# Sums of weight blocks made by accumulating transfers on GpSimd's queue instead of by VectorE

## The chip, the cores and the metric

One NeuronCore of a Trainium2 chip runs the whole program. The metric is the device time of one execution in microseconds (us), the median of three runs. Beside it stands one profiled execution with a time of its own. All data are float32. The core has TensorE (PE) for matrix products, VectorE (DVE), ScalarE (ACT) and GpSimd (POOL) for elementwise work, SyncE (SP) that issues most transfers, and 16 DMA engines that all queues of transfers share.

## What is computed

One decoder layer for 512 tokens of width 1024: half a SwiGLU, a mixer of gated linear attention and dilated attention, half a SwiGLU, and a last norm. The change touches the first two products of each SwiGLU only.

```python
def swiglu(x, w1, w3, w2):
    return (jax.nn.silu(x @ w1) * (x @ w3)) @ w2
x = x + 0.5 * swiglu(rms_norm(x, ffn1_norm[l]), ffn1_w1[l], ffn1_w3[l], ffn1_w2[l])
# ... mixer ...
x = x + 0.5 * swiglu(rms_norm(x, ffn2_norm[l]), ffn2_w1[l], ffn2_w3[l], ffn2_w2[l])
```

The hidden width is 2816, that is 22 tiles of 128 columns for `w1` and 22 for `w3`.

## The kernel before

**Units.** Weights come in units of [128 x 2048] float32, 1 MB each, into two buffers `raw0` and `raw1` that units use in turn. An "up" unit holds one 128-column tile of `w1` and one of `w3` for all 1024 inputs. Each float32 operand is split in a rounded part and the rest (`w_hi` by ACT, `w_lo` = raw - `w_hi` by DVE), and each product is three matmuls. A feed-forward layer runs in two parts of 12 and 10 up units, each followed by 8 "down" units.

**Seven-product units.** 35 of the 44 up units (the table `SEVEN`) are computed by a scheme of seven block products in place of eight. It needs sums of the token blocks, made once per layer (`tok_sums`), and for every such unit four sums of weight blocks. The unit's 2048 columns lie in `raw` as the blocks B22, B21, B11, B12, of 512 columns each. The sums are B22+B21, then that plus B11 (the near pair, for the unit's first side), and B11+B21, and the three-block sum plus B12 (the far pair, for its second side). In before, `add_blocks` makes all four on DVE from `raw`, into the spare columns of the tile `x`, one buffer for all units.

**Order around it.** A seven-product unit has two sides (halves), and `w_hi`, `w_lo` are double-buffered by side. PE works through seven terms of 12 matmuls; term 0 reads raw blocks of side 0 (`w_part`), term 1 is the first that reads sums (`w_split` of side 0), term 4 the first of side 1. While PE works on a unit, ACT and DVE prepare its side 1 and then side 0 of the next unit. For side 0 ACT rounds B11 and B12 (`round_raw`, L592) and the near sums (`round_sums`, L602); for side 1 it rounds B22 (L595) and the far sums (L602). DVE takes the differences (L1059, L1064, L1067), and each L1067 raises `w_split`. Between these, in fixed order on the same queues, ACT copies finished terms out of PSUM (`snap`, L704), and DVE forms gate and product (L1168 to L1187).

**Loads.** SP loads unit u when `w_split` says that unit u-2 is split on both sides, since it used the same `raw` buffer (L488). GpSimd has no transfers; it makes the rotary tables (L555 to L570, after the first 12 up units) and eight products in the mixer (L577).

## Time and profile before

| | us |
|---|---|
| median of 3 runs | 927.59 |
| lowest, highest | 927.41, 927.83 |
| profiled execution, first to last instruction (span) | 925.8 |
| PE busy | 917.7 |
| DVE busy | 676.5 |
| ACT busy | 463.9 |
| GpSimd busy | 49.2 |
| mean DMA rate | 103 GB/s |

Busy time of an engine tells how much it did, not whether anybody waited for it; matmul records overlap, since matmuls are pipelined. So the views that matter are who waited for whom, the rows in order of time inside a unit, and for transfers the time from issue to landing and the share of the 16 engines that a queue's packets took in a stretch.

### The profile page before, as it was taken

To read this page: it belongs to the slowest core of one execution; us is meant where nothing else is said; L and a number is where in the kernel's file an instruction comes from. 1 tells how busy PE (TensorE), PEld (TensorE's weight loads), DVE (VectorE), ACT (ScalarE), POOL (GpSimd) and SP (SyncE) were. 2 spreads that over 40 slices of the span, in tenths; PEclk is the share of its full clock that TensorE was granted. 3 is DMA by queue.
4 is the path that set the end of the run, shared out by engine and by line. 5 is a ranking of instruction groups with operands and counts; after the bars stand their busy time and mean duration, and the time that the engine had idled before them with its cause. 6 is when DMAs were issued, how large, how long until landed. Compare 5 with 4: busy or idle time off the path is not lost.

```text
span 925.8 us, 15011 instructions
## 1 busy us (share of the span) xinstructions
PE 917.7 (99%) x5972; PEld 811.8 (88%) x5972; DVE 676.5 (73%) x1008; ACT 463.9 (50%) x714; POOL 49.2 (5%) x35
## 2 busy tenths in 40 slices
PE   9999999999999999999999999999999999999997
PEld 8889998899999887888777788889998889999885
DVE  6789975379998568654576748779995358999626
ACT  7756541135655336531346965746653115566323
POOL 0100029200000000000022000000000000000000
PEclk9999999999999999999999999999999999999999
DMA  7222233322322242233212022213223322332562
GB/s 296 91 77 107 92 109 104 112 86 95 134 91 87 88 180 96 92 114 105 79 51 87 10 84 91 91 46 137 92 87 130 102 91 92 104 125 92 168 127 92
DMA packets 37711, 95.67 MB, mean 103 GB/s; under 512 B 22928, under 2 KB 24336, under 8 KB 29456
## 3 DMA queue, kind: packets, MB, share of 16 engines
q1 hardware_dynamic: 16224, 91.89, 28.1%
q10 hardware_dynamic: 21424, 2.91, 2.0%
q8 instruction: 44, 0.72, 0.3%
q14 instruction: 19, 0.16, 0.1%
HBM read 90.07 MB, written 2.10 MB: 100 GB/s over the span
## 4 chain that ended last, share of the span: by engine, by line
PE 97%; DVE 1%; issue 1%; ACT 0%; DVEq 0%; ACTq 0%
PE bank L1686 18%; PE bank L1688 17%; PE bank L1687 17%; PE bank L1739 13%; PE bank L1743 13%; PE bank L1741 13%; PE bank L2032 1%; PE bank L2065 1%; PE bank L2048 1%; PE bank L1783 0%; PE bank L1845 0%; PE bank L1789 0%; PE bank L1791 0%; DVE x_tok L1503 0%; DVE w_lo L1028 0%
## 5 line engine op out<-in xcount | busy, mean ns | idle before, releaser
L585 ACT ACTIVATE w_hi<-raw 128x2048 fp32r<-128x2048 f32 (+2 forms) x52 | 87.4, 1680 | 150.1 <-PE bank L1688 138.3
L1739 PE MATMUL bank<-tok_sums,w_hi 128*128 128x256 f32 x560 | 157.9, 282 | 0.0
L1743 PE MATMUL bank<-tok_sums,w_lo 128*128 128x256 f32 x560 | 157.7, 282 | 0.0
L1741 PE MATMUL bank<-tok_sums,w_hi 128*128 128x256 f32 x560 | 157.6, 281 | 0.0
L1028 DVE TENSOR_TENSOR w_lo<-raw,w_hi 128x2048 fp32r<-128x2048 f32 (+2 forms) x52 | 105.4, 2026 | 54.1 <-ACT w_hi L585 53.6
L1743 PE MATMUL bank<-h_both,w_lo 128*128 128x256 f32 x420 | 118.5, 282 | 0.0
L1739 PE MATMUL bank<-h_both,w_hi 128*128 128x256 f32 x420 | 118.4, 282 | 0.0
L1741 PE MATMUL bank<-h_both,w_hi 128*128 128x256 f32 x420 | 118.3, 282 | 0.0
L1686 PE MATMUL bank<-g_hi,w_hi 128*128 128x512 f32 x272 | 105.9, 389 | 0.0
L1739 PEld LDWEIGHTS bank<-tok_sums,w_hi 128*128 128x128 f32 x560 | 105.9, 189 | 0.0
L1688 PE MATMUL bank<-g_hi,w_lo 128*128 128x512 f32 x272 | 105.8, 389 | 0.0
L1687 PE MATMUL bank<-g_lo,w_hi 128*128 128x512 f32 x272 | 105.8, 389 | 0.0
L1741 PEld LDWEIGHTS bank<-tok_sums,w_hi 128*128 128x128 f32 x560 | 105.7, 189 | 0.0
L1743 PEld LDWEIGHTS bank<-tok_sums,w_lo 128*128 128x128 f32 x560 | 105.4, 188 | 0.0
L1686 PE MATMUL bank<-h_both,w_hi 128*128 128x512 f32 x264 | 104.3, 395 | 0.1
L1688 PE MATMUL bank<-h_both,w_lo 128*128 128x512 f32 x264 | 102.9, 390 | 0.0
L1687 PE MATMUL bank<-h_both,w_hi 128*128 128x512 f32 x264 | 102.9, 390 | 0.0
L1067 DVE TENSOR_TENSOR w_lo<-x,w_hi 128x1024 fp32r<-128x1024 f32 x70 | 85.3, 1219 | 0.9 <-ACT w_hi L602 0.9
L704 ACT ACTIVATE masks<-bank 128x256 f32<-128x256 f32 x140 | 53.0, 378 | 64.9 <-PE bank L1743 64.7
L1741 PEld LDWEIGHTS bank<-h_both,w_hi 128*128 128x128 f32 x420 | 79.6, 189 | 0.2
L1743 PEld LDWEIGHTS bank<-h_both,w_lo 128*128 128x128 f32 x420 | 79.7, 190 | 0.0
L1739 PEld LDWEIGHTS bank<-h_both,w_hi 128*128 128x128 f32 x420 | 79.5, 189 | 0.2
(266 smaller groups left out, 1708.2 us busy)
## 6 DMA issues: line engine op xcount, KB each, us to landing
raw<-in_up SPq DMA_DIRECT2D x43, 1024.0 KB, 4.8
raw<-in_w_proj SPq DMA_DIRECT2D x8, 1024.0 KB, 4.9
raw<-in_down1a SPq DMA_DIRECT2D x8, 768.0 KB, 4.2
raw<-in_down2a SPq DMA_DIRECT2D x8, 768.0 KB, 4.2
raw<-in_down1b SPq DMA_DIRECT2D x8, 640.0 KB, 3.8
raw<-in_down2b SPq DMA_DIRECT2D x5, 1024.0 KB, 4.8
raw<-in_w_v SPq DMA_DIRECT2D x4, 1024.0 KB, 4.7
raw<-in_w_o SPq DMA_DIRECT2D x4, 1024.0 KB, 4.8
```

The lines of the kernel that those rows point to most:

```text
L585: nc.scalar.activation(w_hi[slot_of(u)][:, 0:size], raw[u % 2][:, 0:size], ACT.Copy).then_inc(w_round, 1)
L704: nc.scalar.activation(to, where, ACT.Copy).then_inc(snap_taken, 1)
L1028: nc.vector.tensor_tensor(w_lo[slot_of(u)][:, 0:size], raw[u % 2][:, 0:size], w_hi[slot_of(u)][:, 0:size].bitcast(F32), ALU.subtract).then ...
L1067: nc.vector.tensor_tensor(quads(lo[:, at:at + 2 * QUAD]), spare(4 * side, 4 * side + 4), quads(hi[:, at:at + 2 * QUAD]).bitcast(F32), ALU. ...
L1686: nc.tensor.matmul(out, a_hi, b_hi, start=first, stop=False)
L1687: nc.tensor.matmul(out, a_hi, b_lo, start=False, stop=False)
L1688: return nc.tensor.matmul(out, a_lo, b_hi, start=False, stop=last)
L1739: nc.tensor.matmul(out, hi[:, cols], both[:, 0, :], start=start and p == 0, stop=False, skip_group_check=True)
L1741: nc.tensor.matmul(out, hi[:, cols], both[:, 1, :], start=False, stop=False, skip_group_check=True)
L1743: last = nc.tensor.matmul(out, lo[:, cols], both[:, 0, :], start=False, stop=p == PAIRS - 1, skip_group_check=True)
L2032: last = nc.tensor.matmul(ps[4 + e][:, cols.start + c * width:cols.start + (c + 1) * width], projT[r:r + HD, T_AQ + 2 * p, i * P:(i + 1) * P],
L2048: last = nc.tensor.transpose(ps[2 + e][:, j * P:(j + 1) * P], probs[s % PROB_BUFS][e][:, j * P:(j + 1) * P], ident)
```

## The change

All four sums leave DVE. SP loads, beside the unit's 1 MB, two copies of blocks of 512 KB each into a buffer of sums: `load_near` brings B22 and B11, `load_far` brings B11 and B12. GpSimd then issues four accumulating transfers (the destination gets destination + source), each over 256 KB: B21 from HBM onto the first block (`near_two`), the first onto the second (`near_three`), B21 from HBM onto the third (`far_two`), the second onto the fourth (`far_four`). There are two buffers, used in turn by seven-product units: the new `block_sums`, and the spare columns of `x`. ACT now waits for the landing semaphores instead of `w_sums`.

```diff
@@ SyncE @@
             def load(u, i, src):
+                if u in sevens:
+                    load_near(u, src)
                 if not (isinstance(i, int) and u + 2 * i < 2):
                     sp.wait_ge(w_split, split_count(u - 2) if isinstance(i, int) else first_half[u] - 1 + 2 * i)
                 sp.dma_start(raw[u % 2][:, 0:src.shape[-1]], src).then_inc(w_in[u % 2], 16)
+                if u in sevens:
+                    load_far(u, src)
+            def load_near(u, src):
+                s = sevens.index(u)
+                for r in sums_before(s):
+                    sp.wait_ge(w_split, first_half[sevens[r]] + 1)
+                    sp.wait_ge(far_four[sums_slot(s)], sums_landed(r))
+                if sums_slot(s):
+                    sp.wait_ge(sums_ready, PAIRS * (1 if u < U_MIX else 2))
+                blocks = src.rearrange("p (b h a f) -> p b h a f", b=2, h=2, a=2)[:, :, 0, :, :]
+                sp.dma_start(block_sum(s, 0, 4).rearrange("p (b a) f -> p b a f", a=2),
+                             blocks).then_inc(near_in[sums_slot(s)], 16)
+            def load_far(u, src):
+                s = sevens.index(u)
+                for r in sums_before(s):
+                    sp.wait_ge(w_split, first_half[sevens[r]] + 2)
+                sp.dma_start(block_sum(s, 4, 8), src[:, B11_AT:B11_AT + 2 * QUAD].rearrange("p (a f) -> p a f", f=2 * P)
+                             ).then_inc(far_in[sums_slot(s)], 16)
@@ GpSimd @@
+            def add_blocks(u, src):
+                s = sevens.index(u)
+                j, count = sums_slot(s), sums_landed(s)
+                b21 = src[:, B21_AT:B21_AT + QUAD].rearrange("p (a f) -> p a f", f=2 * P)
+                pool.wait_ge(near_in[j], count)
+                pool.dma_start(block_sum(s, 0, 2), b21, accum_op=ALU.add).then_inc(near_two[j], 16)
+                pool.wait_ge(near_two[j], count)
+                pool.dma_start(block_sum(s, 2, 4), block_sum(s, 0, 2), accum_op=ALU.add).then_inc(near_three[j], 16)
+                pool.wait_ge(far_in[j], count)
+                pool.dma_start(block_sum(s, 4, 6), b21, accum_op=ALU.add).then_inc(far_two[j], 16)
+                pool.wait_ge(near_three[j], count)
+                pool.dma_start(block_sum(s, 6, 8), block_sum(s, 2, 4), accum_op=ALU.add).then_inc(far_four[j], 16)
@@ ScalarE @@
             def round_sums(u, side):
-                act.wait_ge(w_sums, 4 * sevens.index(u) + 4)
+                s = sevens.index(u)
+                act.wait_ge((far_four if side else near_three)[sums_slot(s)], sums_landed(s))
+                if side:
+                    act.wait_ge(far_two[sums_slot(s)], sums_landed(s))
@@ VectorE @@
-            def add_blocks(u):
...
@@ program @@
-    nc = bacc.Bacc("TRN2", target_bir_lowering=False, num_devices=1)
+    nc = bacc.Bacc("TRN2", target_bir_lowering=False, num_devices=1, dynamic_dma_scratch_size=2048)
```

GpSimd's additions for the first up part stand behind its first two rotary instructions, those of the second part behind the tables, those of the second layer behind its mixer products.

VectorE, in the middle of an up part. Before, one unit's rows (`x` are the sums, `raw0` the unit's blocks, `bank2` a finished tile):

```order
L1043 TENSOR_TENSOR x<-raw0 128x2x256 [waits w_split,sums_ready,w_in0]
L1044 TENSOR_TENSOR x<-raw0 128x2x256
L1046 TENSOR_TENSOR x<-x,raw0 128x2x256 [waits w_sums]
L1048 TENSOR_TENSOR x<-x,raw0 128x2x256 [waits w_sums]
L1187 TENSOR_TENSOR g_lo1<-prod1,g_hi1 128x512 [waits g_round]
L1059 TENSOR_TENSOR w_lo1<-raw0,w_hi1 128x1024 [waits w_part_round,g_ready]
L1067 TENSOR_TENSOR w_lo1<-x,w_hi1 128x1024 [waits w_round]
L1168 TENSOR_TENSOR gate1<-bank2,masks 128x512 [waits snap_taken,tile_done]
```

The same place after:

```order
L1236 TENSOR_TENSOR g_lo1<-prod1,g_hi1 128x512 [waits g_round]
L1114 TENSOR_TENSOR w_lo1<-raw0,w_hi1 128x1024 [waits w_part_round,g_ready]
L1122 TENSOR_TENSOR w_lo1<-x,w_hi1 128x1024 [waits w_round]
L1217 TENSOR_TENSOR gate1<-bank2,masks 128x512 [waits snap_taken,tile_done]
L1219 TENSOR_TENSOR gate1<-gate1,rstd 128x512 [waits tile_out]
```

The four additions are gone; the rest stands in the same order.

GpSimd after, two units in a row (before, nothing stands between its rotary instructions):

```order
L604 DMA block_sums<-in_up1 128x512 [waits near_in0]
L606 DMA block_sums<-block_sums 128x512 [waits near_two0]
L608 DMA block_sums<-in_up1 128x512 [waits far_in0]
L610 DMA block_sums<-block_sums 128x512 [waits near_three0]
L604 DMA x<-in_up1 128x2x256 [waits near_in1]
L606 DMA x<-x 128x2x256 [waits near_two1]
L608 DMA x<-in_up1 128x2x256 [waits far_in1]
L610 DMA x<-x 128x2x256 [waits near_three1]
```

Each unit's four transfers stand in one in-order queue, and the next unit's first stands behind the fourth.

SyncE after, two units in a row; before, each of these units had the `raw` row alone:

```order
L525 DMA block_sums<-in_up1 128x2x512 [waits far_four0,w_split]
L512 DMA raw1<-in_up1 128x2048 [waits w_split]
L533 DMA block_sums<-in_up1 128x1024 [waits w_split]
L525 DMA x<-in_up1 128x4x256 [waits sums_ready,far_four1,w_split]
L512 DMA raw0<-in_up1 128x2048 [waits w_split]
L533 DMA x<-in_up1 128x4x256 [waits w_split]
```

The load of `raw` now stands behind the near load, and so behind its waits.

## Rows read from the trace of the kernel before

**Rows 1.** The page: the span, busy time by engine, granted clock in 40 slices.

```profile
span 925.8 us, 15011 instructions
PE 917.7 (99%) x5972; PEld 811.8 (88%) x5972; DVE 676.5 (73%) x1008; ACT 463.9 (50%) x714; POOL 49.2 (5%) x35
PEclk9999999999999999999999999999999999999999
```

**Rows 2.** Waits of PE, whole span: line, releaser, total us, times, longest.

```profile
PE bank L1845 <- DVE rope_c L1281: 1.1, 1, 1.1
PE bank L1686 <- issue: 0.2, 1, 0.2
```

**Rows 3.** Windows: us, busy PE, PEld, DVE, ACT, POOL (instructions), clock, DMA share, GB/s.

```profile
216.00:226.00 10.00, 10.00 (x86) 10.00 (x85) 9.68 (x15) 6.05 (x10) 0.00 (x0) 1.00 0.30 107
226.00:236.00 10.00, 10.00 (x86) 10.00 (x85) 9.68 (x15) 6.05 (x10) 0.00 (x0) 1.00 0.29 105
```

**Rows 4.** DVE's groups by line, two of the four additions: busy us, mean ns.

```profile
L1043 DVE TENSOR_TENSOR x<-raw 128x512 f32<-128x512 f32 x35 | 23.9, 683 | 0.5
L1046 DVE TENSOR_TENSOR x<-x,raw 128x512 f32<-128x512 f32 x35 | 24.2, 692 | 1.2
```

**Rows 5.** SP in order of time: start us, us, issues of loads.

```profile
175.51 8.42 SPq L488 DMA_DIRECT2D raw<-in_up  x2
200.07 0.33 SPq L488 DMA_DIRECT2D raw<-in_up  x1
220.06 0.33 SPq L488 DMA_DIRECT2D raw<-in_up  x1
230.06 0.33 SPq L488 DMA_DIRECT2D raw<-in_up  x1
```

**Rows 6.** ACT in order of time, one unit: start us, us, idle before.

```profile
234.01 1.05 ACT L602 ACTIVATE w_hi<-x 128x1024 fp32r<-128x1024 f32 x1
236.58 0.63 ACT L595 ACTIVATE w_hi<-raw 128x512 fp32r<-128x512 f32 x1 [1.52 <-PE bank L1743]
237.12 1.04 ACT L602 ACTIVATE w_hi<-x 128x1024 fp32r<-128x1024 f32 x1
```

**Rows 7.** DVE in order of time, the same unit.

```profile
235.13 1.22 DVE L1067 TENSOR_TENSOR w_lo<-x,w_hi 128x1024 fp32r<-128x1024 f32 x1
238.81 1.22 DVE L1067 TENSOR_TENSOR w_lo<-x,w_hi 128x1024 fp32r<-128x1024 f32 x1
```

**Rows 8.** PE in order of time: the first matmul of that unit that reads sums.

```profile
237.81 0.28 PE L1739 MATMUL bank<-tok_sums,w_hi 128*128 128x256 f32 x1
```

**Rows 9.** Transfers by line: count, KB each, median us from issue to landing.

```profile
raw<-in_up SPq DMA_DIRECT2D x43, 1024.0 KB, 4.8
x_tok<-x_blocks ACTq DMA_DIRECT2D x16, 128.0 KB, 3.4
out<-x_tok SPq DMA_DIRECT2D x6, 256.0 KB, 2.0
k_tok<-k_blocks ACTq DMA_DIRECT2D x16, 32.0 KB, 2.0
x<-in_final_gain SPq DMA_DIRECT2D x1, 512.0 KB, 5.8
```

**Rows 10.** DMA view of 220 to 230 us (one load): SP's queue, share of 16 engines.

```profile
q1 hardware_dynamic: 144, 1.05, 29.5%
```

**Rows 11.** DMA view of 864.6 to 872 us: one load and the final gain.

```profile
q1 hardware_dynamic: 672, 1.57, 59.1%
```

**Rows 12.** DMA view of 910.8 to 912.9 us: stores of 256 KB.

```profile
q1 hardware_dynamic: 241, 0.46, 56.4%
```

**Rows 13.** Issue on SP (ns min, median, max); GpSimd's groups by line (mean ns).

```profile
L488 SPq DMA_DIRECT2D raw<-in_up x43: 327/328/517, 4.5 to 837.8; - x43
L561 POOL TENSOR_SCALAR masks<-masks 128x512 f32<-128x512 f32 x2 | 4.8, 2416 | 0.2
L570 POOL TENSOR_SCALAR rope_c<-rope_c 128x512 f32<-128x512 f32 x1 | 2.0, 2002 | 0.1
L570 POOL TENSOR_SCALAR rope_s<-rope_s 128x512 f32<-128x512 f32 x1 | 0.6, 613 | 0.1
```

More of the change, by code:

```diff
@@ L252, in layer_program @@
         w_part = sem("w_part")
-        w_sums = sem("w_sums")
+        near_in = [sem(f"near_in{j}") for j in range(2)]
+        far_in = [sem(f"far_in{j}") for j in range(2)]
+        near_two = [sem(f"near_two{j}") for j in range(2)]
+        far_two = [sem(f"far_two{j}") for j in range(2)]
+        near_three = [sem(f"near_three{j}") for j in range(2)]
+        far_four = [sem(f"far_four{j}") for j in range(2)]
         seven_half = sem("seven_half")
@@ L408, in spare, with sums_slot, sums_landed, sums_before @@
             return x[:, lo:hi:step, S:S + 2 * P]
+        def sums_slot(s):
+            return (s - sum(u < U_FFN2 for u in sevens)) % 2 if sevens[s] >= U_FFN2 else s % 2
+        def sums_landed(s):
+            return 16 * sum(sums_slot(r) == sums_slot(s) for r in range(s + 1))
+        def sums_before(s):
+            return [r for r in range(s) if sums_slot(r) == sums_slot(s)][-1:]
+        def block_sum(s, lo, hi):
+            return spare(lo, hi) if sums_slot(s) else block_sums[:, lo:hi, :]
         def last_bank(t, half):
@@ L571, in _ @@
                 last.then_inc(ang_sin, 1)
+            add_phase(0, PARTS[1][0], up1)
             for n in range(2 * ST):
@@ L602, in round_sums @@
                 nc.scalar.activation(hi[:, at:at + 2 * QUAD].rearrange("p (a f) -> p a f", f=2 * P),
-                                     spare(4 * side, 4 * side + 4), ACT.Copy).then_inc(w_round, 1)
+                                     block_sum(s, 4 * side, 4 * side + 4), ACT.Copy).then_inc(w_round, 1)
             def round_half(m):
@@ L1066, in low_half @@
                 at = QUAD if side else 2 * QUAD
-                nc.vector.tensor_tensor(quads(lo[:, at:at + 2 * QUAD]), spare(4 * side, 4 * side + 4),
+                nc.vector.tensor_tensor(quads(lo[:, at:at + 2 * QUAD]), block_sum(s, 4 * side, 4 * side + 4),
                                         quads(hi[:, at:at + 2 * QUAD]).bitcast(F32), ALU.subtract).then_inc(w_split, 1)
-            def split_half(m):
-                u, side = halves[m]
-                if u in sevens and side == 0:
-                    add_blocks(u)
-                low_half(m)
             def split_next(u, i):
@@ L1217, in up_phase @@
                                     low_pair(layer, pairs[0])
-                                if seven:
-                                    v, side = halves[first_half[u0 + f] + 2]
-                                    summed = v in sevens and side == 0
-                                    if summed:
-                                        add_blocks(v)
                                 low_g(f - 1)
```

29 lines of the change are left out of this document (9 added, 20 removed).

## The prediction

> **What bounds the kernel.** Begin with the page: PE is busy for 917.7 of 925.8 us at full granted clock [rows 1]. Then see whether it ever waits. It does so twice, for 1.3 us in all, both at single places outside the steady part [rows 2]. Inside a seven-product stretch, ten-microsecond windows read the same: PE 10.00, DVE 9.68, ACT 6.05, and the DMA engines 0.30 busy [rows 3]. DVE is nearly full there, which invites relief, but it is never late. So the kernel runs at PE's pace, and a change that leaves the matmuls alone can gain only what DVE keeps from PE, which is nothing in these rows. It can lose as soon as the new way delivers sums later than PE uses them. The question is one of deadlines.
>
> **What is removed.** Four additions of 0.68 to 0.69 us per unit [rows 4], 2.75 us of DVE in 10, and 96 us over 35 units. PE never waits for DVE there, so I cost this at nothing. ACT's and DVE's other work stays in its order.
>
> **What the sums must meet.** Take the unit whose load SP issues at 220.06 [rows 5]. ACT rounds its near sums at 234.01, DVE takes the difference at 235.13 and is done at 236.35 [rows 6, 7], and PE first reads the result at 237.81 [rows 8]. So near sums may land 1.46 us later than 234.01 before PE waits: 15.4 us after the load's issue. (Those 1.46 us also fit into ACT's idle 1.52 us ahead of L595 [rows 6].) The far sums are rounded at 237.12, 17.1 us after the issue. The load waits for the previous L1067 of side 1; side 0's L1067 lies 3.7 us earlier [rows 7], and that frees the near load, so in the new kernel it starts 3.7 us ahead of the load of `raw`.
>
> **What is added on SP and the DMA engines.** Per unit, two more loads of 512 KB and four additions of 256 KB. SP's issue takes 0.33 us [rows 13]; three in 10 us are harmless. `raw` stands behind the near load, which waits for `far_four` of two units earlier, 20 us back; covered. Engine time: a load of 1 MB takes 29.5% of 10 us, 2.95 us [rows 10]. The final gain, 512 KB in rows of 1 KB, takes 59.1% of 7.4 us less that load, 1.42 us [rows 11]. A plain copy of 256 KB takes 56.4% of 2.1 us for 0.46 MB, so 0.67 us [rows 12]. If an addition cost what a copy costs, a unit would use 2.95 + 2 x 1.42 + 4 x 0.67 = 8.5 us of the engines in PE's 9.99. But an addition must read its destination as well as its source; I take twice a copy, 1.35 us each, and get 11.2 us. No row shows such a transfer: the near bound is one copy, the far bound four.
>
> The Trainium skill, page Collectives: The Full Stack, section "The bandwidth ceiling: the fold count and why AG ≠ RS ≠ AR", says that a reducing transfer emits two reads per chunk and so runs at half a copy's rate; by it an addition is 1.35 us and by the copy rows alone 0.67. No row here can show it.
>
> **What is added on GpSimd's queue.** This is where I look for the bound. The queue is in order: `near_two` of a unit, a wait until it landed, `near_three`, `far_two`, a wait until `near_three` landed, `far_four`, and then the next unit's `near_two`. So each unit costs two full steps from issue to landing and one more issue, and no two units overlap, however many buffers there are. A step: 1.8 us fixed (a 32 KB copy in SBUF lands after 2.0 us, with little of its own to move [rows 9]), 1.35 of its own, and GpSimd's issue, which no row shows. SP's is 0.33; GpSimd's instructions of 512 columns are 0.6 to 2.4 us [rows 13]. I take 1.0, that is 0.7 more than the fixed part holds, near SP's end. That is 3.9 us alone. It is not alone: `near_two` meets the load of `raw` (2.95 us of the same engines) and `near_three` the far load (1.42). If they alternate packet by packet, the first is lengthened by about 2.4 and the second by 1.4, on average 1.9. A loaded step is 5.8 us; bounds are 2.0 (the 256 KB store [rows 9]) and about 9. The unit's circle is 2 x 5.8 + 1.0 = 12.6 us, against PE's 9.99 (the distance of loads [rows 5]): an excess of 2.6 us per unit.
>
> **The sum.** The near load starts 3.7 us ahead of `raw` and lands about 3.2 us later (fixed 1.8 and 1.42), at -0.5 us by the load's issue. Near sums land at -0.5 + 11.6 = 11.1, against 15.4: a reserve of 4.3 us. The first two units of each part have more: their loads are issued at 175.5 and 183.6, the third's at 200.1, and the others follow by 10 [rows 5]. So the excess counts from the third unit on. With 7, 10, 8 and 10 such units in the four parts, that is 4 + 7 + 5 + 7 = 23 excesses, 59.8 us, less four reserves, 17.2 us: 42.6 us. The span becomes 968.4 us. The median of the runs stands 1.8 us above the profiled span (927.6 against 925.8), which gives **970 us**.
>
> Two moved things cost nothing more. The rotary tables stand behind the first part's additions, but start late anyway and have some 25 us to spare before the second part's sevens; and the second layer's additions stand behind the mixer's GpSimd products, long done by then.
>
> **Rivals.** *No change, 927.6 us.* An addition costs a copy's 0.67 us, and GpSimd issues nearly as fast as SP. The loaded step is then 1.8 + 0.67 + 1.9 = 4.4 us or less, the circle 9.1, the engines 8.5: both under 9.99, and PE never notices. Because the reserve of 4.3 us is spread over seven units, it decides at a loaded step of about 5.0 us; over it the kernel is slower. For it: landings of 2.0 us for 256 KB, and engines 70% idle. Against it: it needs both unknowns at their cheap end. Chance 0.27.
>
> *The DMA engines are the bound, 1005 to 1080 us.* If an addition takes as much as three copies, a unit needs 2.95 + 2.84 + 8.0 = 13.8 us, with four 16.5. The excess is 3.8 to 6.5 us, times 23 gives 87 to 150, less what is left of the reserves at the low end. Chance 0.18. For it: I know of no row with an addition, and small packets cost more per byte (1.42 us for 512 KB in 1 KB rows against 2.95 for 1 MB). Against: the queue waits long enough between its transfers to leave the engines pauses.
>
> *GpSimd held up by DVE, 1045 us.* The same GpSimd operation, L570, took 0.61 us once and 2.00 once, both while DVE worked [rows 13]; nothing else in the trace tells the two apart. If its issue of a transfer is stretched to 2.0 us in the same way, a step is 6.8 us, the circle 15.6, the excess 5.6 and the reserve 2.3: 23 x 5.6 - 4 x 2.3 = about 118 us. DVE would be busy two thirds of the time in the new kernel, so it would not strike every issue. Chance 0.08. The Trainium skill, page SBUF — State Buffer, section "🔬 SBUF: two separate sides", warns of this: DVE instructions in a mode with two ports keep GpSimd from writing descriptors, and its transfers stall. The section "Who interferes with whom" excepts the adding and subtracting of two tensors, which is what DVE runs here; by it this rival would hardly occur.
>
> *Faster, 923.5 us.* PE's whole idle time is 8.1 us [rows 1]. DVE with 96 us less work could give back at most about half of it at the seams. Against: no wait of PE for DVE in an up part [rows 2]. Chance 0.03.
>
> **Chances and range.** The forecast, GpSimd's serial circle with 930 to 1004 us, has 0.44, and 970 lies near its middle. A measurement of this kernel tells about 0.2% from no change, 1.9 us. Faster 0.03, same 0.27, slower 0.44 + 0.18 + 0.08 = 0.70. The forecast's own range is 935 to 1000. The range for 8 in 10 takes in no change and the lower half of the engine-bound rival: 927 to 1040.
>
> **What would show it.** In the changed profile PE should wait in up parts, from the third or fourth seven-product unit on and then in every one, for ACT's rounding of sums, and ACT in turn for `near_three` or `far_four`. Each part's units should lie about 12.6 us apart late in the part and 10 early. From issue to landing GpSimd's four transfers should read near 5 to 6 us, and its queue should have one waiting for the other all the time. DMA share in the stretch should be 0.8 to 0.9. If it reads 1.0 with landings over 7 us, the engines are the bound; if landings are under 5 us and PE does not wait, it is the first rival. DVE should lose 96 us of busy time in all cases. If PE waits so long that its granted clock falls, the loss is larger than the sum; no row of before bears on that. What makes it wrong most easily is the size of a loaded step: 0.5 us of it is 1.0 us of excess, 23 us of the time.

## The result, and the profile after

The changed kernel takes **1055.3 us** (median; 1048.3 to 1057.5), the kernel before 927.6 beside it. The ratio is 1.1365, 95% interval 1.1347 to 1.1383: 128 us slower, three times the forecast loss and outside the range. Of all kernels below only x9 had executions in the chip's slower state, two of its four, and its time is given by the other two. The profiled execution's span is 1055.5 us, 129.7 above that of before. The page of the changed kernel, which answers [rows 1] and [rows 10]; its last line is the chain of work that ended last, by engine, which was 97% PE before:

```profile
span 1055.5 us, 15114 instructions
PE 957.4 (91%) x5972; PEld 840.9 (80%) x5972; DVE 591.5 (56%) x868; ACT 464.2 (44%) x714; POOL 196.7 (19%) x175
PEclk9997999999899999999999999989999999888999
q1 hardware_dynamic: 41664, 128.59, 36.0%
q0 software_dynamic: 28864, 36.71, 22.2%
PE 44%; DMA 41%; DVE 5%; issue 4%; ACT 4%; POOL 2%; SPq 0%; ACTq 0%; DVEq 0%; POOLq 0%
```

The span's 129.7 us are on PE's side: 90.0 of idle time (1055.5 - 957.4 = 98.1 against 8.1) and 39.7 of matmuls that last longer. Its waits, which answer [rows 2] (line, releaser, total us, times, longest):

```profile
PE bank L1778 <- DVE w_lo L1122: 48.6, 17, 5.6
PE bank L1778 <- ACT masks L775: 41.1, 26, 3.6
```

L1778 is the matmul. L1122 is the difference that splits the sums, the old L1067. L775 is ACT's copy of finished term 0 out of PSUM; it stands behind the rounding of far sums in ACT's queue, and ACT is held up there. So both rows lead to ACT's rounding, L673, and that waits for transfers (waits of ACT):

```profile
ACT w_hi L673 <- DMA x<-x: 96.1, 28, 7.1
ACT w_hi L673 <- DMA block_sums<-block_sums: 60.2, 21, 5.1
```

The transfers by tile, KB and median us from issue to landing, which answer [rows 9] (POOLq is GpSimd's queue):

```profile
raw<-in_up SPq DMA_DIRECT2D x43, 1024.0 KB, 6.3
block_sums<-in_up SPq DMA_DIRECT2D x36, 512.0 KB, 7.2
x<-in_up SPq DMA_DIRECT2D x34, 512.0 KB, 7.5
block_sums<-in_up POOLq DMA_DIRECT2D x36, 256.0 KB, 6.3
block_sums<-block_sums POOLq DMA_DIRECT2D x36, 256.0 KB, 4.9
x<-in_up POOLq DMA_DIRECT2D x34, 256.0 KB, 8.5
x<-x POOLq DMA_DIRECT2D x34, 256.0 KB, 5.3
```

These rows mix transfers of different kinds. The same by line of the program, in this order: near load, far load, `near_two`, `near_three`, `far_two`, `far_four`:

```profile
DMA to landing us min/median/max: 3.5/3.8/10.7
DMA to landing us min/median/max: 6.5/8.8/12.6
DMA to landing us min/median/max: 3.7/5.3/11.4
DMA to landing us min/median/max: 3.3/6.8/10.2
DMA to landing us min/median/max: 3.5/9.2/10.7
DMA to landing us min/median/max: 3.3/4.2/9.6
```

So the near load is not late: it lands after 3.8 us. The forecast's 5 to 6 us fits `near_two` alone.

One window, as in [rows 3]: clock 0.91, DMA share 0.90, 209 GB/s:

```profile
216.00:296.00 80.00, 66.86 (x476) 64.18 (x475) 39.21 (x53) 32.29 (x53) 20.95 (x21) 0.91 0.90 209
```

GpSimd's queue in order of time shows the circle of two units (L604 is `near_two`, L606 `near_three`, L608 `far_two`, L610 `far_four`):

```profile
249.66 1.40 POOL L604 DMA_DIRECT2D block_sums<-in_up  x1
254.85 0.87 POOL L606 DMA_DIRECT2D block_sums<-block_sums  x1 [3.80 <-DMA block_sums<-in_up]
255.41 1.22 POOL L608 DMA_DIRECT2D block_sums<-in_up  x1
261.94 0.86 POOL L610 DMA_DIRECT2D block_sums<-block_sums  x1 [5.30 <-DMA block_sums<-block_sums]
262.51 1.51 POOL L604 DMA_DIRECT2D x<-in_up  x1
268.29 1.20 POOL L606 DMA_DIRECT2D x<-x  x1 [4.26 <-DMA x<-in_up]
269.02 1.73 POOL L608 DMA_DIRECT2D x<-in_up  x1
273.82 1.21 POOL L610 DMA_DIRECT2D x<-x  x1 [3.08 <-DMA x<-x]
274.55 1.42 POOL L604 DMA_DIRECT2D block_sums<-in_up  x1
```

One unit's circle is 12.9 us here, the next 12.0. Over the middle units of all parts the mean is 15.3: 7.0 from `near_two` to `near_three`, 7.7 from there to `far_four`, 0.6 to the next `near_two`. **This pace is the whole loss.** Summed over the 31 distances inside the four parts, the `near_two`s lie 483 us apart in the changed kernel. In a kernel that takes 927.5 us (x12 below) the same 31 distances are 353 us. The difference is 131 us, and the span lost 129.7. This tells where the loss lies. Which of the coupled queues leads is for the experiments to tell.

SP now waits too, and not for a short time (waits of SP's queue; L521 and L523 stand for the near load into the one buffer and the other):

```profile
SPq L523 <- DMA x<-x: 143.8, 13, 13.5
SPq L521 <- DMA block_sums<-block_sums: 121.0, 12, 11.1
```

The forecast had called this wait, for `far_four` of the same buffer, covered. It is not. But GpSimd's wait for the near load (L604 is `near_two`) is rare, 6 times in 35 units:

```profile
POOL block_sums L604 <- DMA block_sums<-in_up: 132.8, 3, 74.3
POOL x L604 <- DMA x<-in_up: 27.3, 3, 13.0
```

So in most units the near load has landed before GpSimd comes to it. Four theories were therefore tested. A: the serial circle on GpSimd's queue. B: the engines' load. C: PE's clock. D: the loop of two units through the sums' buffer and SP's wait for `far_four`. In the later runs E stands for B in terms of steps, F for the fixed part of a transfer, G for D, and R for the order in GpSimd's ring.

### The profile page after: what moved, and what is told of

It is laid out like the page before. It is cut to its first block, busy times and chain, and to the rows that moved or that the text cites. A ratio compares the mean times of both kernels' runs of the same rounds, so it can differ in the third digit from the quotient of the medians.

```text
span 1055.5 us, 15114 instructions
## 1 busy us (share of the span) xinstructions
PE 957.4 (91%) x5972; PEld 840.9 (80%) x5972; DVE 591.5 (56%) x868; ACT 464.2 (44%) x714; POOL 196.7 (19%) x175
## 3 DMA queue, kind: packets, MB, share of 16 engines
q0 software_dynamic: 28864, 36.71, 22.2%
## 4 chain that ended last, share of the span: by engine, by line
PE 44%; DMA 41%; DVE 5%; issue 4%; ACT 4%; POOL 2%; SPq 0%; ACTq 0%; DVEq 0%; POOLq 0%
DMA x<-x 12%; DMA x<-in_up 12%; PE bank L1725 12%; PE bank L1727 11%; PE bank L1726 11%; DMA block_sums<-in_up 8%; DMA block_sums<-block_sums 7%; PE bank L1778 2%; PE bank L1780 2%; PE bank L1782 2%; DVE w_lo L1099 1%; ACT w_hi L653 1%; PE bank L2071 1%; PE bank L2104 1%; POOL x L610 1%
## 5 line engine op out<-in xcount | busy, mean ns | idle before, releaser
L1778 PE MATMUL bank<-tok_sums,w_hi 128*128 128x256 f32 x560 | 173.9, 311 | 89.9 <-DVE w_lo L1122 48.6
L1778 PEld LDWEIGHTS bank<-tok_sums,w_hi 128*128 128x128 f32 x560 | 115.6, 207 | 100.1 <-DVE w_lo L1122 52.0
L1782 PE MATMUL bank<-tok_sums,w_lo 128*128 128x256 f32 x560 | 167.5, 299 | 0.0
L1780 PE MATMUL bank<-tok_sums,w_hi 128*128 128x256 f32 x560 | 167.5, 299 | 0.0
L1778 PE MATMUL bank<-h_both,w_hi 128*128 128x256 f32 x420 | 121.1, 288 | 0.0
L1780 PE MATMUL bank<-h_both,w_hi 128*128 128x256 f32 x420 | 120.6, 287 | 0.0
L1780 PEld LDWEIGHTS bank<-tok_sums,w_hi 128*128 128x128 f32 x560 | 116.4, 208 | 0.0
L1782 PEld LDWEIGHTS bank<-tok_sums,w_lo 128*128 128x128 f32 x560 | 116.0, 207 | 0.0
L1778 PEld LDWEIGHTS bank<-h_both,w_hi 128*128 128x128 f32 x420 | 82.7, 197 | 0.2
L1780 PEld LDWEIGHTS bank<-h_both,w_hi 128*128 128x128 f32 x420 | 82.4, 196 | 0.2
L1782 PEld LDWEIGHTS bank<-h_both,w_lo 128*128 128x128 f32 x420 | 82.2, 196 | 0.0
L775 ACT ACTIVATE masks<-bank 128x256 f32<-128x256 f32 x140 | 52.7, 377 | 62.9 <-PE bank L1782 62.9
L673 ACT ACTIVATE w_hi<-x 128x1024 fp32r<-128x1024 f32 x34 | 35.9, 1056 | 96.1 <-DMA x<-x 96.1
```

The costliest lines, as they stand in the source:

```text
L673: nc.scalar.activation(hi[:, at:at + 2 * QUAD].rearrange("p (a f) -> p a f", f=2 * P), block_sum(s, 4 * side, 4 * side + 4), ACT.Copy).the ...
L775: nc.scalar.activation(to, where, ACT.Copy).then_inc(snap_taken, 1)
L1778: nc.tensor.matmul(out, hi[:, cols], both[:, 0, :], start=start and p == 0, stop=False, skip_group_check=True)
L1780: nc.tensor.matmul(out, hi[:, cols], both[:, 1, :], start=False, stop=False, skip_group_check=True)
L1782: last = nc.tensor.matmul(out, lo[:, cols], both[:, 0, :], start=False, stop=p == PAIRS - 1, skip_group_check=True)
```

## Experiments

Each kernel is the changed one with one edit, timed beside the kernel before. Of the edits the main lines are shown. Medians are of 4 runs (10 for x1 and x12); x1 and x10 to x14 were chosen after the others. "Circle" is the mean distance of `near_two` issues over the middle units of the parts, by the start times on GpSimd; "engine work" is the shares of q0 and q1 from the page times the span, (22.2% + 36.0%) x 1055.5 = 614 us in the changed kernel.

### x12_one_of_four: one sum by transfer, three on DVE

```diff
-    (near load 512 KB, far load 512 KB, four additions)
+    sp.dma_start(block_sum(s, 0, 2), <B22 of the unit>)                # 256 KB
+    pool.dma_start(block_sum(s, 0, 2), b21, accum_op=ALU.add)          # near_two
+    nc.vector.tensor_tensor(<the other three sums>)
```

> Only the first sum (B22 + B21) is made by a transfer, from one load of 256 KB and one addition; VectorE makes the other three. Engine time per unit is 2.95 + 0.7 + 1.4 = 5.0 us of 10. If what counts is the share of the engines that a unit needs, this fits: 926 to 930 us, landing of the addition 4 to 5 us, DVE some 20 us less busy than in the kernel before. If even one addition on the path comes late, 935 us or more with PE waits behind DVE's wait for it. Nobody expects it below 923.

Measured: 927.45 us (927.16 to 927.95), ratio 1.0000 (0.999 to 1.001). DVE is busy 651.7 us, 25 less than before, and PE's waits are those of [rows 2]. Engine work is (31.8% + 6.0%) x 926.2 = 350 us against 260 before. The window of 216 to 296 us:

```profile
216.00:296.00 80.00, 80.00 (x674) 80.00 (x674) 71.53 (x104) 49.49 (x79) 6.32 (x6) 1.00 0.50 138
```

The addition lands after 6.6 us in the median, although the engines are half idle over the window and nothing else is in its queue. It was expected after 4 to 5. It meets the load of `raw`, which SP issues at the same time (both at 221.24 us in one unit). No one is late for it, since PE never waits. So one accumulating transfer does no harm here, and DVE's relief is worth nothing.

### x1_loads_only: the loads without the additions

```diff
-                pool.dma_start(...)                 # all four additions of a unit
+                return
-                act.wait_ge((far_four if side else near_three)[...], ...)
+                act.wait_ge((far_in if side else near_in)[...], ...)
```

> Of the changed kernel all three loads of a unit stay, and all four additions go: ACT rounds the loaded blocks themselves, so the sums are left out. Engine time falls to 2.95 + 2 x 1.42 = 5.8 us of 10. If it is the additions (their engine time and their serial order) that cost the 128 us, nothing is left: 926 to 930 us, PE without waits, near and far loads landing after 4 to 5 us. If the two extra loads by themselves come too late (SP's queue, collisions with the unit's load), some of it stays: 940 us or more, with PE waiting.

Measured: 927.53 us (927.15 to 928.08), ratio 1.0001 (0.9992 to 1.0011). SP's queue has 39.2% of 925.8 us on the page. The window of 216 to 236 us:

```profile
216.00:236.00 20.00, 20.00 (x171) 20.00 (x170) 14.56 (x21) 12.10 (x20) 0.00 (x0) 1.00 0.59 211
```

Near and far loads land after 4.0 and 5.9 us in the median. SP's wait for `far_four` is gone too. Engine work is 363 us, so the two extra loads cost 363 - 260 = 103 us or 2.9 per unit: the 2 x 1.42 of the forecast is right, and twice the old engine share is free. The 128 us belong to the additions.

### x2_independent: four additions that don't depend on each other

```diff
-                pool.wait_ge(near_two[j], count)
-                pool.dma_start(block_sum(s, 2, 4), block_sum(s, 0, 2), accum_op=ALU.add)...
+                pool.dma_start(block_sum(s, 2, 4), b21, accum_op=ALU.add)...
                 pool.wait_ge(far_in[j], count)
                 pool.dma_start(block_sum(s, 4, 6), b21, accum_op=ALU.add)...
-                pool.wait_ge(near_three[j], count)
-                pool.dma_start(block_sum(s, 6, 8), block_sum(s, 2, 4), accum_op=ALU.add)...
+                pool.dma_start(block_sum(s, 6, 8), b21, accum_op=ALU.add)...
```

> The changed kernel with the same two loads and four additions of 256 KB per seven-product unit, but none of the additions waits for another: each adds B21 from HBM onto its block, so three of the sums are other sums than the reference's. Theory A (the serial circle on GpSimd's queue, two steps from issue to landing and one issue per unit, sets the pace of 14 to 15 us): the circle is gone, only the DMA engines' own 11 to 12 us per unit are left against 9.99 of PE, so 950 to 980 us. Theory B (the DMA engines are saturated by these bytes): nothing changes, 1045 to 1060 us.

Measured: 984.65 us (981.4 to 985.0), ratio 1.0617 (1.0599 to 1.0635). The window of 216 to 296 us:

```profile
216.00:296.00 80.00, 74.31 (x583) 73.50 (x582) 48.82 (x67) 41.70 (x68) 29.67 (x28) 0.94 1.04 265
```

B21 is added where the chain's sums were, so bytes, packets and engine work (601 us) are nearly the same, and the engines read full at 1.04. Circle 12.6 us: the pace of full engines with this work. `near_two` waits for the near load in 24 of 35 units here, so SP's wait for `far_four` is part of this pace. The dependences among the additions cost the other 71 us. Theory A came nearer than B, but 985 is above its 980, for full engines alone cost 57 us.

### x3_near_chain_only: the serial pair alone

```diff
-                pool.wait_ge(far_in[j], count)
-                pool.dma_start(block_sum(s, 4, 6), b21, accum_op=ALU.add)...              # far_two
                 pool.wait_ge(near_three[j], count)
-                pool.dma_start(block_sum(s, 6, 8), block_sum(s, 2, 4), accum_op=ALU.add)... # far_four
```

> The changed kernel without the two far additions (the far blocks are rounded as loaded, so those sums are left out); the near chain and the two loads stay. GpSimd waits for the second near addition before it goes on. Theory A: the circle is two steps, each shorter by the lighter traffic, about 4 to 5 us: 9 to 10 us per unit, 927 to 950 us. Theory B: the engines need 8.3 us per unit, 927 to 930 us, with landings near the unloaded 3.3 to 3.7 us.

ACT rounds the far blocks as loaded, and SP no longer waits for `far_four`. Measured: 976.37 us (970.6 to 981.5), ratio 1.0531 (1.0477 to 1.0585). Both forecasts were too low. Circle 12.3: 5.6 us from `near_two` to `near_three` and 6.7 to the next unit's `near_two`. With just one addition in flight at a time, two waits for landing are already more than PE's 9.99. This is nearly the circle that the prediction had computed for all four, and in part by chance, for it had counted on more traffic.

### x4_pipelined: the next unit's near_two ahead of far_four

```diff
-                for f in SEVEN[layer, a]:
-                    add_blocks(part_unit(layer, a) + f, up[f + a])
+                for n, f in enumerate(units):
+                    add_blocks(unit f, ..., 0)              # near_two
+                    if n > 1: add_blocks(unit f - 1, ..., 2) # far_two, far_four of the unit before
+                    add_blocks(unit f, ..., 1)              # near_three
```

> The changed kernel, same transfers and same dependences, but GpSimd issues them in another order: first near addition of a unit, then both far additions of the unit before, then the second near addition, so that only one landing is waited for per unit. Theory A: the circle shrinks to one step of 6 to 9 us, the engines' 11 to 12 us are left, 950 to 990 us. Theory B: 1045 to 1060 us.

Measured: 1057.86 us (1053.4 to 1061.6), ratio 1.1418 (1.1393 to 1.1444): no gain, and in the range that was written for theory B. Circle 15.1. The steps became longer as the order became looser: 8.1 us to `near_three`. GpSimd's order of instructions alone is not the cause.

### x7_near_load_split: B22 loaded without the wait for far_four

```diff
-                    sp.wait_ge(far_four[sums_slot(s)], sums_landed(r))
-                sp.dma_start(block_sum(s, 0, 4)..., blocks)
+                sp.dma_start(block_sum(s, 0, 2), <B22>)
+                    sp.wait_ge(far_four[sums_slot(s)], sums_landed(r))
+                sp.dma_start(block_sum(s, 2, 4), <B11>)
```

> The changed kernel with the near load split in two of 256 KB: B22 goes as soon as side 0 of the unit two before is split, and only B11, whose place far_four still reads, waits for far_four to land. Theory D (the loop over a buffer of sums: near load, near_two, near_three, far_four, and then the near load of the unit after next, 29.9 us for two units, sets the pace): a load's landing and one step leave the loop, which becomes some 20 to 24 us for two units, so 965 to 1010 us. Theory A (GpSimd's queue alone: from one unit's near_two to the next one's 15 us): nothing changes, 1045 to 1060 us.

Measured: 1075.1 us (1072.4 to 1080.9), ratio 1.1606 (1.1565 to 1.1647): slower by 20 us, outside both forecasts. `near_three` also waits for B11. Circle 16.2. SP's wait is only moved: `raw` stands behind it as before.

### x8_split_and_pipelined: both

> The split near load and the other order on GpSimd's queue together; same additions, bytes and dependences as in the changed kernel. If the pace is set by two loops that each need to be cut (the buffer's and the queue's, theory A+D): near the time of the kernel whose additions were independent, 975 to 1000 us, while either cut alone gives little. Theory D alone: the same as the split alone. If it is the engines' capacity and nothing else: 1045 to 1060 us.

The edit is that of x4 and that of x7 together. Measured: 1041.71 us (1041.1 to 1044.7), ratio 1.1243 (1.1224 to 1.1262), circle 14.2. This is between the forecasts. Both loops opened give 14 us of 128.

### x11_no_near_load: the loop through SP taken away

```diff
-                if u in sevens:
+                if u in sevens and not sums_before(sevens.index(u)):
                     load_near(u, src)
-                pool.wait_ge(near_in[j], count)
+                    pool.wait_ge(w_split, first_half[sevens[r]] + 1)
+                    pool.wait_ge(far_four[j], sums_landed(r))
```

> The near load is left out for all but the first unit of each buffer (the sums then add onto what lies there), and GpSimd itself waits until the buffer is free, so SP's queue no longer waits for far_four and raw is issued as in the kernel before. Engine time falls by 1.4 of about 13 us. Theory G (the loop through SP's wait for far_four is what turns 12.6 into 15.3 us a unit): the units come 12.5 to 13 us apart or less, 965 to 985 us. Theory A/B (GpSimd's serial circle on loaded engines alone): steps fall only in the ratio of the engines' load, to about 6.3 and 6.9, units 14 us apart, 1010 to 1035 us.

Measured: 1035.72 us (1035.0 to 1037.7), ratio 1.1173 (1.1154 to 1.1191). SP's 265 us of waits for `far_four` are gone, and still the circle is 15.2, with steps of 7.8 and 6.7. That is just above the forecast of the serial circle (1010 to 1035). The near load's landing, and SP's wait for `far_four`, are effects of the pace and set at most the 20 us that this edit returned.

### x10_half_chain: the same chain with half the bytes

```diff
-                pool.dma_start(block_sum(s, 0, 2), b21, accum_op=ALU.add)...
+                pool.dma_start(block_sum(s, 0, 1), b21[:, 0:1, :], accum_op=ALU.add)...
                 (and so for the other three)
```

> The same four additions in the same order with the same waits, each over half of its block (128 KB, the other half of each sum is left out). The engines' time per unit falls by about 3.3 of 13 us; the number of transfers, issues and waits stays. Theory E (a step's length is mostly waiting and moving on loaded engines): steps of 7.0 and 7.7 us fall to about 4.5, the circle 10 to 10.5 us, time 930 to 955. Theory F (it is the fixed part of four dependent transfers on one queue): steps stay near 7, time over 1000 us.

Measured: 974.33 us (969.8 to 978.8), ratio 1.0502 (1.0458 to 1.0546). Engine work falls from 614 to 504 us, the loss from 128 to 47, between the two forecasts: the circle is 12.3, the step after `near_three` fell from 7.7 to 4.3, but the step from `near_two` to `near_three` stayed at 7.2. In this kernel the load of `raw` is in flight during every `near_two` from the third unit of a part on, as the table below shows, where in the changed kernel it is so in 9 units of 23. So the step that lost bytes of its own met more of another's.

### x13 and x14: order in the ring, or work on the engines

What stands ahead of a transfer in its own queue can be told from the landings in the trace ("ring" below is the queue of GpSimd's packets). Over the 23 units from the third on of each part, `near_two` takes 6.5 us from issue to landing. For 4.6 of these the previous unit's `far_four`, ahead of it in the same queue, has not landed; then come 1.9 more. `near_three` has nothing ahead of it and takes 7.2. The queue view of the changed kernel from 249.6 to 254.9 us, one `near_two` from issue to release, fits this (packets, MB, share):

```profile
q0 software_dynamic: 416, 0.52, 63.3%
q1 hardware_dynamic: 118, 0.12, 10.7%
```

GpSimd's queue moved 0.52 MB, two additions and not one. The Trainium skill, page DMA: Bandwidth & Descriptors, section "Two DMAs through the same engine are not ordered", says that the descriptors of one queue start in order on each engine. The trace fits it: each of 34 `near_two`s landed after the `far_four` ahead of it, and the row shows 0.52 MB against the 0.26 of `near_two`. The forecast had `near_two` meet only the load of `raw`.

The next step of the same unit, `near_three` from 254.85 to 261.9 us, is filled from the other side:

```profile
q1 hardware_dynamic: 689, 1.59, 60.6%
q0 software_dynamic: 183, 0.34, 38.9%
```

SP issued `raw` at 255.69 and the far load at 256.06, just behind `near_three`, and its queue moved 1.59 MB in the step, 4.3 us of the 16 engines. The forecast had `near_three` meet the far load alone, 1.42 us. In all 23 units both loads were in flight during `near_three`. The means over the 23 units, with the engine time that the packets of each queue took between issue and landing:

| kernel, step | us to landing | GpSimd's queue, us | SP's queue, us |
|---|---|---|---|
| after, `near_two` | 6.5 | 3.8 | 1.8 |
| after, `near_three` | 7.2 | 2.4 | 4.4 |
| x3, `near_two` | 5.1 | 1.6 | 2.4 |
| x3, `near_three` | 6.2 | 1.7 | 3.8 |
| x10, `near_two` | 7.0 | 2.1 | 3.7 |
| x10, `near_three` | 4.0 | 1.2 | 2.2 |
| x12, `near_two` | 6.4 | 1.6 | 2.8 |

These columns tell what the engines did in a step; a longer step also takes in more. Two kernels were made to tell the order in the ring from the bare load on the engines. In x13 ACT and SP wait as in x3; in x14 they wait for `far_two` in place of `far_four`:

```diff
@@ x13, on x3_near_chain_only @@
+                    for e in range(2):     # HBM to HBM, 512 KB each, on SP's queue
+                        sp.dma_start(aside[...][:, :, 0:2 * P], src[...])...
@@ x14, on the changed kernel @@
-                pool.dma_start(block_sum(s, 6, 8), block_sum(s, 2, 4), accum_op=ALU.add)...  # far_four
```

> The kernel with near_two and near_three alone (far sums left out), and beside it, per unit, two plain copies of 512 KB in 1 KB rows from HBM to HBM, on SyncE's queue behind the far load: 2 x 1.42 = 2.8 us of engine time if they cost what the final gain's row shows, as much as far_two and far_four (2.7). Theory R (order in GpSimd's ring: near_two stands behind far_four): the ring holds only the two additions, steps stay near 5.6 to 6, units 12.3 to 12.8 us apart, 975 to 990 us. Theory E (the engines' total work): the total is that of the changed kernel, steps 7 us, units 14.5 to 15.3 apart, 1030 to 1055 us.

> The changed kernel without far_four (the fourth sum is left out; ACT and SP wait for far_two in its place). GpSimd's circle still waits for near_two and near_three. Theory R: near_two now stands behind only the rest of far_two, about 2 us instead of 3.9; a step of 5.2 to 5.8 and one of 6.9, units 12.5 to 13 us apart, 975 to 995 us. Theory E: engine time per unit falls from about 13 to 11.6 us and the steps with it, 6.3 and 6.9, units 13.6 to 14 apart, 1005 to 1025 us.

Measured for x13: 1037.44 us (1031.0 to 1039.8), ratio 1.1178 (1.1129 to 1.1228). Its queues on the page:

```profile
q1 hardware_dynamic: 78624, 165.30, 47.4%
q0 software_dynamic: 14432, 18.35, 11.5%
```

And its GpSimd in order of time (L609 is `near_two`, L611 `near_three`):

```profile
270.96 0.90 POOL L609 DMA_DIRECT2D block_sums<-in_up  x1 [8.41 <-DMA x<-x]
275.10 0.86 POOL L611 DMA_DIRECT2D block_sums<-block_sums  x1 [3.24 <-DMA block_sums<-in_up]
279.81 1.23 POOL L609 DMA_DIRECT2D x<-in_up  x1 [3.85 <-DMA block_sums<-block_sums]
288.08 1.21 POOL L611 DMA_DIRECT2D x<-x  x1 [7.04 <-DMA x<-in_up]
298.91 0.90 POOL L609 DMA_DIRECT2D block_sums<-in_up  x1 [9.62 <-DMA x<-x]
```

The ring holds only the serial pair, the engines the work of the changed kernel (58.9% x 1033.3 = 609 us), and 61 of the 79 us between x3 and the changed kernel are back. The theory of the ring's order alone falls. But the steps are uneven, 4.1 and 4.7 us, then 8.3 and 10.8, and the mean circle is 13.7, not 15.3. So with one addition at a time in the ring a step can still be twice another. One caution: the copies (which land after 10.0 us) also stand ahead of the next near load in SP's queue, so x13 may lose a little by a way of its own.

Measured for x14: 1003.88 us (1003.3 to 1005.1), ratio 1.0825 (1.0807 to 1.0843), circle 13.1, steps of 6.5 and 6.6, engine work 559 us. The time is just below the forecast of load (1005), the circle nearer that of order (12.5 to 13). `far_four` alone costs 51 us, though nobody on GpSimd waits for it. ACT does, so the edit also takes a deadline away: PE's waits behind ACT's copy of term 0 fall from 41.1 to 8.5 us.

### x5_two_and_two: two sums by transfer, two on DVE

```diff
-                pool.wait_ge(near_two[j], count)
-                pool.dma_start(block_sum(s, 2, 4), block_sum(s, 0, 2), accum_op=ALU.add)...
-                pool.wait_ge(near_three[j], count)
-                pool.dma_start(block_sum(s, 6, 8), block_sum(s, 2, 4), accum_op=ALU.add)...
+                nc.vector.tensor_tensor(block_sum(s, 2, 4), block_sum(s, 2, 4), block_sum(s, 0, 2), ALU.add)
+                nc.vector.tensor_tensor(block_sum(s, 6, 8), block_sum(s, 6, 8), block_sum(s, 2, 4), ALU.add)
```

> Only the two additions of B21 from HBM (near_two, far_two) are transfers; near_three and far_four are VectorE additions of 0.69 us again, all sums as in the reference. GpSimd never waits for a landing, the engines need 8.3 us per unit. Theories A and D: one step in place of three, PE never waits, 927 to 932 us. If any added traffic of this size is harmful: over 940 us.

Measured: 955.08 us (947.9 to 957.9), ratio 1.0279 (1.0231 to 1.0328); the forecast of no loss failed. Engine work is 493 us, the window's share 0.82; `near_two` lands after 7.7 us in the median and `far_two` after 5.0. Here no addition waits for another one. DVE, which makes the far sum (L1109), waits for `far_two` in six units:

```profile
DVE x L1109 <- DMA x<-in_up: 19.0, 6, 4.3
```

PE waits 18.8 us, for ACT's copy of term 0. That DVE's waits for `far_two` are the cause of the whole 27 us is not shown.

### x6 and x9: is PE's clock a cost of its own?

39.7 us of the loss are matmuls that last longer. Three windows show how: PE busy 7.80 of 7.80 us at full clock, then, after a wait of 2.7 us, a stretch at 0.50, that is 1.2 GHz in place of 2.4, then full clock again:

```profile
271.60:279.40 7.80, 7.80 (x68) 7.80 (x67) 4.78 (x6) 3.19 (x5) 2.15 (x2) 1.00 1.06 271
281.80:288.60 6.80, 6.17 (x29) 6.17 (x30) 3.19 (x5) 2.91 (x7) 3.04 (x4) 0.50 0.92 244
288.60:309.10 20.50, 15.75 (x130) 15.35 (x130) 9.89 (x13) 8.54 (x14) 5.34 (x5) 1.00 0.87 204
```

In all, 77 us of the span ran at half clock; before, it was the last 4 us alone. Two kernels ask whether that adds to the time: x6 gives PE 20 useless matmuls in each seven-product unit, half of them ahead of the wait for split sums; x9 leaves out one of the three matmuls of each product in the seven-product units, 117 us of PE's work.

```diff
@@ x6 @@
+                        fill()                  # 10 matmuls of 256 columns
                         pe.wait_ge(w_split, m + 1)
                         term(gates[:, right], 0, 2 * QUAD, summed(0), start=True)
+                        fill()
@@ x9 @@
-                                nc.tensor.matmul(out, hi[:, cols], both[:, 1, :], start=False, stop=False, ...)
```

> The changed kernel with 20 matmuls of 256 columns more per seven-product unit on PE, 10 (1.2 us) ahead of each of the two places where PE waits (sums of side 0; the copy of term 0); their result is not used. Theory C (some 40 of the 128 us lost come from the granted clock, which falls to half in 15 stretches after PE has waited): the work fills waits of 2.6 us per unit, the clock stays up, PE's stretches at half clock go from 75 us to under 20, and the time falls by 15 to 35 us, to 1015 to 1040, although 83 us of work are added. If the clock costs nothing: no change or up to 20 us more, 1055 to 1075.

> The changed kernel without one of the three matmuls of every product in the seven-product units (rounded weights by low token half is left out): 28 matmuls or 3.3 us less PE work per unit, 117 us in all. If the loop of transfers alone sets the pace (A or D): PE only waits longer, 1040 to 1060 us. If PE's own work or its lowered clock is part of what sets the pace: up to 80 us less, 975 to 1035 us.

Measured for x6: 1109.72 us (1103.5 to 1110.5), ratio 1.1944 (1.1907 to 1.1982). The stretches at half clock stayed at 76 us, so the filling did not do what it was made for. It only added work and 54 us. Both forecasts (1015 to 1040, 1055 to 1075) failed, and the run says nothing for or against the clock. Measured for x9: 1048.2 and 1059.5 us, about the changed kernel's own 1048.3 to 1057.5. PE was busy 882.2 us, 75 less than in the changed kernel, its granted clock was lower (0.896 in the mean against 0.963, with 218 us at half clock against 77), and the circle was 15.3 again. So neither PE's work nor its clock sets the time. The reading that fits is that half clock fills time that PE would else have spent waiting.

### The experiments side by side

| kernel | engine work, us | additions a unit waits for in turn | us | over before |
|---|---|---|---|---|
| before | 260 | none | 927.6 | |
| x12 one of four | 350 | 1 | 927.5 | 0 |
| x1 loads only | 363 | none | 927.5 | 0 |
| x3 near chain only | 492 | 2 | 976.4 | 49 |
| x5 two and two | 493 | 1 | 955.1 | 27 |
| x10 half the bytes | 504 | 2 | 974.3 | 47 |
| x14 no far_four | 559 | 2 | 1003.9 | 76 |
| x11 no near load | 561 | 2 | 1035.7 | 108 |
| x2 independent | 601 | none of the other | 984.7 | 57 |
| x13 near chain and copies | 609 | 2 | 1037.4 | 110 |
| after | 614 | 2 and far_four behind them | 1055.3 | 128 |

Among kernels with the serial pair, the loss grows with the engines' work, whoever it is for: 47 to 49 us at about 500, 76 and 108 at 560, 110 and 128 at 609 and 614. (Work is not all: x14 and x11 differ by 32 us at the same work, and x11 has all four additions in its ring, x14 three.) At the same work of 600 to 614 it is 57 without the dependence and 110 to 128 with it.

## Why the prediction was wrong in size and right in direction

**Right.** PE bound the kernel and DVE's relief was worth nothing (x12, x1). The loss is paid through deadlines of the sums, from GpSimd's queue with its two serial steps; PE waits for ACT's rounding, and ACT for `near_three` and `far_four`. The DMA share is 0.90 where 0.8 to 0.9 was forecast, but by luck: work and circle were both larger than forecast, some 13.8 us of 15.3 in place of 11.2 of 12.6. Two loads take 2.9 us a unit of engine time (2.84 taken). An addition costs 234 / 140 = 1.67 us of the engines (22.2% of 1055.5 over 140 additions) and 1.65 in x3 (11.9% of 972.5 over 70), where twice a copy, 1.35, was taken; the cheap end of 0.67 is out. An addition's packet of 1 KB takes 102 ns in the median and a load's 46, one of 2 KB 178 and 84: 2.1 to 2.2 times, that is near a half of a copy's rate. That is the rule of the Trainium skill, page Collectives: The Full Stack, section "The bandwidth ceiling: the fold count and why AG ≠ RS ≠ AR", that the prediction cites; it holds for these transfers. GpSimd's issue lasts 0.86 to 1.73 us (rows above), where 1.0 was taken; the unloaded step fits as well, its shortest landings being 3.3 to 3.7 us against 3.9 with the issue.

**The step that failed: "a loaded step is 5.8 us".** It is 7.0 and 7.7 us from one issue to the next, the circle 15.3, not 12.6. The term had each addition meet one load: `near_two` that of `raw` (2.4 us more), `near_three` the far load (1.4 us more). The packets show other meetings. `near_two` is queued behind the two far additions of the unit before in the same ring, "nobody waits for them" being true of GpSimd's instructions and not of its packets: for 4.6 of its 6.5 us `far_four` has not landed, and GpSimd's queue takes 3.8 us of the engines in it, where its own addition costs 1.67. `near_three` meets the load of `raw` and the far load together, 4.4 us of the engines in place of 1.42. With one addition in flight (x3) the steps are 5.6 and 6.7. x13 shows that the ring's order is not all of it: the same work on another queue brings most of the loss back. How much of the 2.7 us comes from the order in the ring and how much from sharing busy engines stays open. In terms of the sum: 23 units x (15.3 - 9.99) = 122 us in place of 59.8.

**The second: a reserve of 4.3 us in each part.** The near load was to land 3.2 us after its issue, and `near_two` to start then. The load does land after 3.8 us. But GpSimd is still at the unit before: `near_two` is issued 10.6 us after the near load in the mean of the 23 units, and already 6.7 to 18.1 us after it in the third unit of each part. By the prediction's own count the near sums then come at 10.6 - 3.7 + 2 x 7.35 = 21.6 us after the load's issue, against a deadline of 15.4. The 17.2 us of reserves don't exist. Then 122 us and the units ahead of the third in each part, which were taken as free, make up the 130.

**The third, smaller: "`far_four` two units earlier, 20 us back; covered".** With a circle of 15.3 that is no longer so, and SP waits 265 us. x11 shows that this is mostly an effect: without the wait and the load the time falls by 20 us only. Nor does `near_two` wait for the near load in most units.

**The rivals.** The bound on engines came nearest by its time, 1005 to 1080, and was right in part: 57 us of the 128 are full engines (x2). But its price was wrong (an addition as three copies or four; it was 1.67 / 0.67 = 2.5), and alone it gives 985. The rule that the prediction gave for telling it, landings over 7 us with a share of 1.0, holds for most of x2's transfers (1.04, medians 6.4 to 9.7 us) and not for the changed kernel. Its remark that small packets cost more per byte is not what its two rows say: 1.42 us for 512 KB is 2.84 for 1 MB, against 2.95. GpSimd held up by DVE: its 1045 us and its circle of 15.6 come near by luck, for in the changed kernel an issue never took 2.0 us, but 0.85 to 1.74 (in x2, whose queue is fuller, the longest took 2.3). The exception for additions of two tensors, which the prediction cites from the Trainium skill, page SBUF — State Buffer, section "Who interferes with whom", agrees with these durations. DVE lost 85 us of busy time, not 96; its records overlap by some 0.1 us each (L1043 starts at 230.62, L1044 at 231.22, with 0.68 us each), which takes up part of it. The clock did fall; that this adds to the loss, as the prediction's last part said, is contradicted by x9 for this kernel.

The range failed because the forecast and its price for the engines were treated as alternatives, each with its own share of chance. The runs side by side speak for one mechanism: a serial circle whose steps stretch with the engines' load.

## What to carry to other kernels

Price a chain of dependent transfers by landing time at the load that the change itself creates, and count for each transfer everything ahead of it in its own ring, also what nobody waits for. A share of 0.5 to 0.6 of the DMA engines was free here (x12, x1) and one of 0.8 or more was not, long before 1.0. The share does not give the landing time: x12's addition took 6.6 us at a share of 0.50, because it met a load of 1 MB, and was free because nobody needed it sooner. Look at which transfers are in flight together, and expect this to shift when the pace does. Where an engine has slack but the DMA engines are to take its work, move one operation, not four, and ask first whether that engine's relief is worth anything: here it was worth nothing.

## What was unexpected of the hardware

- An accumulating transfer of 256 KB costs 1.65 to 1.67 us of the 16 engines, 2.5 times the 0.67 us of the plain copy of before, and GpSimd's issue of it takes 0.86 to 1.73 us.
- Landing times are long before the engines are full: an accumulating transfer of 256 KB lands after 3.3 to 3.7 us at the least, after 6.6 in the median of x12 at a share of 0.50, and after 4.2 to 9.2, by kind, in the changed kernel at 0.90.
- `near_three`, with nothing ahead of it in its ring, still took 7.2 us in the changed kernel, with 4.4 us of the engines given to SP's loads: an empty ring is no protection from other queues on the same engines.
- Opening a loop can cost: x7 took a wait from GpSimd's path and was 20 us slower. Which collision does it was not found.
- PE with 75 us less busy time (x9) had the lower granted clock, 0.896, at about the same time.
